# A short-convolution stage in which high and low inputs are one 512-column product per weight tile

## The reference

```python
def short_conv_mixer(h, w_in, conv_w, w_out):
    b_gate, c_gate, u = jnp.split(h @ w_in, 3, axis=-1)
    v = c_gate * u
    y = sum(conv_w[k] * causal_shift(v, CONV_WIDTH - 1 - k) for k in range(CONV_WIDTH))
    return (b_gate * y) @ w_out

def gated_post_add(x, y, g_post, gate, weight):
    return x + weight * gate[:, None, :] * rms_norm(y, g_post)
```

## Time and profile before

| | us |
|---|---|
| runs | 2331.2, 2337.23, 2337.64 |
| median | 2337.23 |
| the profiled execution | 2332.65 |
| its span in the profile | 2330.9 |
| TensorE busy | 2247.9 (96% of the span) |
| VectorE busy | 1524.1 (65%) |
| ScalarE busy | 974.8 (42%) |
| edited stage, first product to last | about 253.6 to 346 |
| mean granted clock of TensorE | 0.976 |

### The profile page before, as it was taken

How to read it: one execution, slowest core, us unless ns; L and a number is a source line. 1 busy time by engine, 2 the same in 40 slices (tenths; PEclk the granted TensorE clock), 3 DMA queues, 4 the chain that set the end, 5 groups by cost and what they waited for, 6 DMA issues and landing times.

```text
span 2330.9 us, 42281 instructions
## 1 busy us (share of the span) xinstructions
PE 2247.9 (96%) x18080; PEld 2211.7 (95%) x18080; DVE 1524.1 (65%) x1704; ACT 974.8 (42%) x957; POOL 145.4 (6%) x269
## 2 busy tenths in 40 slices
PE   6999999999999998799999999999999999999998
PEld 5999999999999998599999999999999999999997
DVE  6876568877457864768867444758985445666554
ACT  3433444434333343543444444334444444334442
POOL 0110001110001100011100000001100000000000
PEclk8999999999789997999999999999999999999999
DMA  9997457995469942049974544548984544444552
GB/s 329 347 340 244 140 184 273 332 326 174 131 212 335 332 139 91 1 164 341 329 244 162 167 137 167 173 160 290 367 293 154 185 140 163 163 157 164 185 181 72
DMA packets 264592, 494.67 MB, mean 212 GB/s; under 512 B 17041, under 2 KB 146449, under 8 KB 264209
## 3 DMA queue, kind: packets, MB, share of 16 engines
q1 hardware_dynamic: 229760, 366.47, 46.7%
q0 software_dynamic: 34704, 126.37, 14.6%
HBM read 491.73 MB, written 1.05 MB: 211 GB/s over the span
## 4 chain that ended last, share of the span: by engine, by line
PE 92%; DVE 3%; ACT 3%; DMA 1%; issue 1%; SPq 0%; DVEq 0%; ACTq 0%
PE PA L469 15%; PE PA L470 15%; PE PA L471 15%; PE PY L469 7%; PE PY L471 7%; PE PY L470 7%; PE PB L469 5%; PE PB L470 5%; PE PB L471 5%; PE PA L519 2%; PE PB L512 2%; DVE wlo L1257 1%; ACT scr L1141 1%; DVE rstd L1299 1%; PE PY L778 1%; DMA mix<-adat 1%
## 5 line engine op out<-in xcount | busy, mean ns | idle before, releaser
L1257 DVE TENSOR_TENSOR wlo<-raw,whi 128x2048 fp32r<-128x2048 f32 x335 | 764.7, 2286 | 449.6 <-ACT whi L936 342.8
L469 PE MATMUL PA<-opA_hi,whi 128*128 128x256 f32 x2528 | 718.0, 284 | 1.8 <-DVE opA_lo L1310 1.8
L470 PE MATMUL PA<-opA_lo,whi 128*128 128x256 f32 x2528 | 716.8, 284 | 0.0
L471 PE MATMUL PA<-opA_hi,wlo 128*128 128x256 f32 x2528 | 716.7, 284 | 0.0
L936 ACT ACTIVATE whi<-raw 128x2048 fp32r<-128x2048 f32 x203 | 384.9, 1901 | 280.3 <-PE PA L471 139.1
L469 PEld LDWEIGHTS PA<-opA_hi,whi 128*128 128x128 f32 x2528 | 486.7, 193 | 2.5 <-issue 2.5
L470 PEld LDWEIGHTS PA<-opA_lo,whi 128*128 128x128 f32 x2528 | 486.8, 193 | 0.1
L471 PEld LDWEIGHTS PA<-opA_hi,wlo 128*128 128x128 f32 x2528 | 486.8, 193 | 0.0
L469 PE MATMUL PY<-opB_hi,whi 128*128 128x256 f32 x1344 | 381.1, 284 | 9.8 <-DVE opB_lo L1368 6.0
L470 PE MATMUL PY<-opB_lo,whi 128*128 128x256 f32 x1344 | 380.3, 283 | 0.0
L471 PE MATMUL PY<-opB_hi,wlo 128*128 128x256 f32 x1344 | 380.3, 283 | 0.0
(11 more groups left out here) (241 smaller groups left out, 2766.4 us busy)
## 6 DMA issues: line engine op xcount, KB each, us to landing
raw<-ffn_w_in SPq DMA_DIRECT2D x176, 512.0 KB, 5.3
mix<-adat POOLq DMA_DIRECT2D x144, 512.0 KB, 6.5
raw<-w_in SPq DMA_DIRECT2D x144, 512.0 KB, 4.7
raw<-w_ff SPq DMA_DIRECT2D x128, 512.0 KB, 4.6
adaw<-adat POOLq DMA_DIRECT2D x96, 512.0 KB, 6.7
raw<-ffn_w_out SPq DMA_DIRECT2D x88, 512.0 KB, 4.6
raw<-w_branch SPq DMA_DIRECT2D x48, 512.0 KB, 4.5
raw<-a_w_in SPq DMA_DIRECT2D x24, 512.0 KB, 4.5
```

What stands on the lines that cost most here:

```text
L469: nc.tensor.matmul(o_, w1, rhs(xh), start=start, stop=False, skip_group_check=True)
L470: nc.tensor.matmul(o_, w1, rhs(xl), start=False, stop=False, skip_group_check=True)
L471: return nc.tensor.matmul(o_, w2_, rhs(xh), start=False, stop=stop, skip_group_check=True)
L1257: TT(wlo[slot][:, 0:w], raw[slot][:, 0:w], whi[slot][:, 0:w].bitcast(F32), ALU.subtract).then_inc(lo_ready, 1)
```

## The change

- The high and low inputs lie in one tensor `op2` [128, 2, 8, 256]; `oph` and `opl` are views of it.
- In the mixer alone, `pair2` takes the place of `mm3`: whi x [in_hi | in_lo] is one product of 512 columns into one bank. wlo x in_hi, 256 columns, is added to the bank's second half. The first half of a bank then holds the main sum, the second the cross sum, so an output tile takes a whole bank instead of half of one.
- A group of 4 output tiles takes four banks: PA and PB for groups 0, 2, 4 and PY for groups 1, 3, 5. `conv_out` takes all eight and waits for all three buffers.
- Every group is evacuated by ScalarE (the cross half, `conv.c0` to `conv.c5`) and then VectorE (adds the main half, `whole`). The loop on ScalarE goes over all six groups. Groups 3 and 5 land in `tmp8`, and the product with c reads that.
- At the boundary behind it ScalarE copies the cross halves into `cb_` (`conv.yc0` to `yc3`), VectorE adds the main halves (`conv.ys0` to `ys3`), and the squares and the update read `cb_`.

```diff
@@ -143,8 +143,9 @@
         x = sb("x", [P, KT, T])
-        oph = {"A": sb("opA_hi", [P, KT, T], F32R), "B": sb("opB_hi", [P, KT, T], F32R)}
-        opl = {"A": sb("opA_lo", [P, KT, T], F32R), "B": sb("opB_lo", [P, KT, T], F32R)}
+        op2 = {"A": sb("opA", [P, 2, KT, T], F32R), "B": sb("opB", [P, 2, KT, T], F32R)}
+        oph = {n: t_[:, 0] for n, t_ in op2.items()}
+        opl = {n: t_[:, 1] for n, t_ in op2.items()}
         tmp8 = sb("tmp8", [P, KT, T])
@@ -167,6 +168,13 @@
         flat = {k: v[:].rearrange("p a b -> p (a b)") for k, v in PS.items()}
+
+        def bank(i):
+            n, j = ("A", i) if i < 2 else ("B", i - 2) if i < 4 else ("Y", i - 4)
+            return flat[n][:, 512 * j:512 * j + 512]
+
+        def halves(n, half):
+            return PS[n][:].rearrange("p (m h) t -> p m h t", h=2)[:, :, half, :]
 
@@ -626,13 +634,40 @@
 
+            def pair2(c, tile, kts, banks, op, before=None, tag=None):
+                pe.wait_ge(lo_ready, c + 1)
+                slot = c % RING
+                for kk, k in enumerate(kts):
+                    if before:
+                        before(k)
+                    for m, b_ in enumerate(banks):
+                        w_ = slice(tile(kk, m), tile(kk, m) + P)
+                        nc.tensor.matmul(bank(b_), whi[slot][:, w_], op2[op][:, :, k, :], start=k == 0, stop=False,
+                                         skip_group_check=True)
+                        last = nc.tensor.matmul(bank(b_)[:, T:2 * T], wlo[slot][:, w_], op2[op][:, 0, k, :], start=False,
+                                                stop=k == KT - 1, skip_group_check=True)
+                        if tag and k == KT - 1 and m in (1, 3, 5):
+                            S(last, f"{tag}.bank{m // 2}")
+                last.then_inc(multiplied, 1)
+
             for g in range(6):
-                buf = "AB"[g % 2]
-                take(buf)
-                group512(CH["conv_in"] + 2 * g, buf, "A", lo_of("01") if g == 0 else None)
-                by(buf, *(("V", f"conv{g}") if g in (3, 5) else ("S", f"conv{g}")))
-            out1024(CH["conv_out"], "B", "01", lambda k: need(pe, "V", f"conv.lo{k // 4}"))
-            by("Y", "V", "01.u7")
+                if g % 2 == 0:
+                    take("A")
+                    take("B")
+                else:
+                    take("Y")
+                for h in range(2):
+                    pair2(CH["conv_in"] + 2 * g + h, tile_in512, range(4 * h, 4 * h + 4),
+                          range(4) if g % 2 == 0 else range(4, 8), "A", lo_of("01") if g == 0 else None)
+                for n_ in ("AB" if g % 2 == 0 else "Y"):
+                    by(n_, "V", f"conv{g}")
+            for n_ in "ABY":
+                take(n_)
+            for q in range(4):
+                pair2(CH["conv_out"] + q, tile_out, (2 * q, 2 * q + 1), range(8), "B",
+                      lambda k: need(pe, "V", f"conv.lo{k // 4}"), tag="01" if q == 3 else None)
+            for n_ in "ABY":
+                by(n_, "V", "01.ysum")
             boundary("01", "02")
@@ -988,7 +1023,15 @@
 
-                if not sub.startswith("b"):
+                if sub == "01":
+                    for q in range(4):
+                        y_there(q)
+                        n_ = "ABYY"[q]
+                        S(AC(cb_[:, 2 * q:2 * q + 2, :], halves(n_, 1)[:, 2 * (q == 3):2 * (q == 3) + 2, :], ACT.Copy), f"conv.yc{q}")
+                    squares(f"{sub}.y", cb_, lambda q: need(act, "V", f"conv.ys{q}"))
+                    root(f"{sub}.y")
+                    prep_to(c_next + 3)
+                elif not sub.startswith("b"):
                     squares(f"{sub}.y", PY, y_there)
@@ -1081,13 +1124,18 @@
             boundary("00", "01", CH["conv_in"], CH["conv_in"])
-            for g in (0, 1, 2, 4):
+            for g in range(6):
                 c = CH["conv_in"] + 2 * g
...
                 act.wait_ge(multiplied, c + 2)
-                dst = cb_ if g < 2 else cc_
                 half_ = g if g < 2 else (g - 2) // 2
-                S(AC(dst[:, 4 * half_:4 * half_ + 4, :], PS["AB"[g % 2]][:], ACT.Copy), f"conv{g}")
+                dst = cb_[:, 4 * half_:4 * half_ + 4] if g < 2 else cc_[:, 4 * half_:4 * half_ + 4] if g in (2, 4) else \
+                    tmp8[:, 4 * half_:4 * half_ + 4]
+                if g % 2 == 0:
+                    S(AC(dst[:, 0:2, :], halves("A", 1), ACT.Copy))
+                    S(AC(dst[:, 2:4, :], halves("B", 1), ACT.Copy), f"conv.c{g}")
+                else:
+                    S(AC(dst, halves("Y", 1), ACT.Copy), f"conv.c{g}")
             prep_to(CH["conv_out"] + 1)
@@ -1320,6 +1368,13 @@
                 prep_to(c_next + 2)
+                ysrc = cb_ if sub == "01" else PY
+                if sub == "01":
+                    for q in range(4):
+                        need(dve, "S", f"conv.yc{q}")
+                        S(TT(cb_[:, 2 * q:2 * q + 2, :], cb_[:, 2 * q:2 * q + 2, :],
+                             halves("ABYY"[q], 0)[:, 2 * (q == 3):2 * (q == 3) + 2, :], ALU.add), f"conv.ys{q}")
+                    seen["V", "01.ysum"] = S.n
                 if not sub.startswith("b"):
@@ -1331,7 +1386,7 @@
                     for k in range(KT):
-                        S(STT(tmp8[:, k, :], PY[:, k, :], G_(sub)[:, k:k + 1], rstd[:], ALU.mult, ALU.mult), f"{sub}.u{k}")
+                        S(STT(tmp8[:, k, :], ysrc[:, k, :], G_(sub)[:, k:k + 1], rstd[:], ALU.mult, ALU.mult), f"{sub}.u{k}")
                         if k > 0:
@@ -1454,14 +1509,27 @@
             need(dve, "G", "cpad")
+            def whole(pos):
+                c = CH["conv_in"] + 2 * pos
+                prep_to(c + 4)
+                need(dve, "S", f"conv.c{pos}")
+                half_ = pos if pos < 2 else (pos - 2) // 2
+                dst = cb_[:, 4 * half_:4 * half_ + 4] if pos < 2 else cc_[:, 4 * half_:4 * half_ + 4] if pos in (2, 4) else \
+                    tmp8[:, 4 * half_:4 * half_ + 4]
+                if pos % 2 == 0:
+                    S(TT(dst[:, 0:2, :], dst[:, 0:2, :], halves("A", 0), ALU.add))
+                    own(S(TT(dst[:, 2:4, :], dst[:, 2:4, :], halves("B", 0), ALU.add), f"conv{pos}"))
+                else:
+                    own(S(TT(dst, dst, halves("Y", 0), ALU.add), f"conv{pos}"))
+
+            whole(0)
+            whole(1)
             for g in range(2):
                 pos = 3 + 2 * g
-                c = CH["conv_in"] + 2 * pos
-                prep_to(c + 4)
-                dve.wait_ge(multiplied, c + 2)
-                need(dve, "S", f"conv{pos - 1}")
+                whole(pos - 1)
+                whole(pos)
                 ts = range(4 * g, 4 * g + 4)
-                own(S(TT(cv_[:, 4 * g:4 * g + 4, 2:258], PB[:], cc_[:, 4 * g:4 * g + 4, :], ALU.mult), f"conv{pos}"))
+                own(S(TT(cv_[:, 4 * g:4 * g + 4, 2:258], tmp8[:, 4 * g:4 * g + 4], cc_[:, 4 * g:4 * g + 4, :], ALU.mult)))
                 for t in ts:
...
```

More of the change, by code:

```diff
@@ L668, in _ @@
             take("A")
-            bh, bl = (oph["B"][:].rearrange("p a b -> p (a b)"), opl["B"][:].rearrange("p a b -> p (a b)"))
+            bh, bl = (oph["B"].rearrange("p a b -> p (a b)"), opl["B"].rearrange("p a b -> p (a b)"))
             for kv in range(2):
@@ L1111, in _ @@
                 S(AC(vtok[br], t3(flat["Y"][:, n_ * 512:n_ * 512 + 512], 2), ACT.Copy), "vtok")
-            bh = oph["B"][:].rearrange("p a b -> p (a b)")
+            bh = oph["B"].rearrange("p a b -> p (a b)")
             tf = tmp8[:].rearrange("p a b -> p (a b)")
@@ L1203, in _ @@
                 need(act, "V", q_ + "rety2")
-                S(AC(oph["B"][:], tmp8[:], ACT.Copy), q_ + "rhi")
+                S(AC(oph["B"], tmp8[:], ACT.Copy), q_ + "rhi")
                 group("p0", 10, "B", half(1, 0), ACT.Copy)
@@ L1220, in _ @@
                 act.wait_ge(multiplied, c + 32)
-                S(AC(oph["B"][:], tmp8[:], ACT.Copy), q_ + "shi")
+                S(AC(oph["B"], tmp8[:], ACT.Copy), q_ + "shi")
                 group("h11", 17, "B", half(0, 1), ACT.Sigmoid, ("V", q_ + "m0.1"))
@@ L1226, in _ @@
                 act.wait_ge(multiplied, c + 40)
-                S(AC(oph["B"][:], tmp8[:], ACT.Copy), q_ + "phi")
+                S(AC(oph["B"], tmp8[:], ACT.Copy), q_ + "phi")
                 group("h21", 21, "B", half(0, 1), ACT.Sigmoid, ("V", q_ + "m1.1"))
@@ L1486, in _ @@
             tf = tmp8[:].rearrange("p a b -> p (a b)")
-            bh, bl = (z["B"][:].rearrange("p a b -> p (a b)") for z in (oph, opl))
+            bh, bl = (z["B"].rearrange("p a b -> p (a b)") for z in (oph, opl))
             dve.wait_ge(cmp_in, 64)
@@ L1650, in _ @@
                 need(dve, "S", q_ + "rhi")
-                S(TT(opl["B"][:], tmp8[:], oph["B"][:].bitcast(F32), ALU.subtract), q_ + "rlo")
+                S(TT(opl["B"], tmp8[:], oph["B"].bitcast(F32), ALU.subtract), q_ + "rlo")
                 prep_to(c + 25)
@@ L1687, in _ @@
                 need(dve, "S", q_ + "shi")
```

(4 more changed lines are left out.)

## The result

The changed kernel takes 2349.97 us in the median (2341.4 to 2352.62, 7 runs) against 2334.83 of the kernel before in the same runs (2328.85 to 2337.64): a ratio of 1.0062, 95% interval 1.0042 to 1.0081, so 14.5 us slower (10 to 19). The forecast was slower by 8.8 us, 2343.7 with a range of 2337 to 2352. Sign and range held; some 60% of the size was named. The changed kernel once more (e5_after_again) has 2347.0 us against 2333.02: 1.0054 (1.0034 to 1.0073).

The account below looks back on a forecast made before the run. TensorE, never stopping in the edited stage, was taken as the bound. Costs of 13.8 us less gains of 5.0 us gave net +8.8 us, so 2343.7 us, with a range of 2337 to 2352.

Parts of the forecast that it names:

- Step 4: Ahead of conv_out: TensorE stops for VectorE's add of group 5, queued behind a late conv.hi0; +8.35 us.
- Step 1: Mixer tiles: one 512-column product replaces two of 256; a tile takes 0.3375 us, a gain of 22.5 ns.
- Step 5: After the stop ahead of conv_out: TensorE's clock falls and some 5.2 us run at half speed; +2.6 us.
- Step 7: Boundary behind conv_out: ScalarE copies four cross halves first and all four squares come after; +2.45 us.
- Steps 2 and 3: Groups 0 to 3: evacuation hidden, 2.9 us gained. Group 4: copy and add delay chunk 10, +0.4 us.
- Step 6: Group 5 and conv_out's products: 32 and 64 cheaper tiles, nothing else ending later; 2.2 us gained.
- The second of cover at chunk 17: Chunk 17's split would end at T5+31.2, TensorE at T5+32.6; without that cover at most 0.6 us on the path.
- no gain in width: Rival: the wide product costs 0.240 us, so only costs remain, +13.8 us, 2348.7 us; chance 0.19.
- Cheapest pair: Rival: a tile takes 0.325 to 0.330 us, both weight loads hidden; +6.0 us, 2340.9 us; chance 0.17.
- free width: Rival: the wide product costs a weight load, 0.120 us, a tile 0.240 us; -13.1 us, 2321.8 us; chance 0.04.
- the stop was made as read: Rival denied this: TensorE waits only for group 5's copy and add, 2.5 us; +0.3 us, 2335.2; chance 0.05.

Follow-up runs that it names:

- e1_hi0_early: The changed kernel with ScalarE writing conv.hi0 right behind the copy of group 4, not of group 5; ratio 1.0018 to the kernel before, stop 2.53 us.
- e9_late_hi0: The kernel before, with ScalarE made to wait for the end of group 5 ahead of conv.hi0; stop 2.50 us, stage 112.31 us.
- after: The profiled execution of the changed kernel, nothing else edited; 2352.62 us.
- e7_double_wide: The changed kernel with the second product of a tile also 512 columns wide; a tile takes 0.453 us, the profiled execution 2371.86 us.
- e6_front_wide: The wide product in groups 0 to 2 alone, the rest as in the kernel before; 2333.71 us, ratio 1.0002, stage 106.61 us.
- e2_no_pool_adds: The changed kernel with POOL's three adds to x at the boundary behind the mixer made by VectorE; one profiled execution, 2339.91 us.
- e8_interleave: e1_hi0_early with ScalarE's copies and squares at the boundary interleaved, two squares behind the last copy; one profiled execution, 2347.74 us.

## Why the prediction was right, and where it was not

- **Step 4, the stop.** Right in mechanism, order and size: 8.29 us against 8.35, ended by the add that was named. e1_hi0_early and e9_late_hi0 show that it has two causes that only together make it long: without the late `conv.hi0` 2.5 us are left, and with it alone it is 2.5 us as well.
- **Step 1, the price of the wide product.** The mis-sized term. The step took the 0.2175 us of a float32 record with 256 columns as that of one product with 512; measured are 0.230 or 0.2367, and a tile of 0.3467 or 0.3533, not 0.3375; the 0.3533 of 96 of the 256 tiles in after, and of 160 in e5_after_again, lies outside the 0.330 to 0.350 of the forecast. The gain is 13.3 or 6.7 ns a tile and not 22.5. The measured price also lies over both figures that the prediction quotes for this product, 216 and 131 ns. float32r pays 13.3 ns a product whatever its width (e7_double_wide), the float32 record 4. The stage's own spacing of 0.120 us for 256 columns had this number in it: 0.1067 for the columns and 0.0133 over. A row of the same kind of operand, split into a part for columns and a fixed part, was the nearer one. With 13.3 ns the sum would have been 13.8 - 3.0 = +10.8, close to the 11.6 measured, but in part by luck: the clock of step 5 cost 1.0 less than forecast and the boundary of step 7 1.5 more.
- **Steps 2 and 3.** Evacuation through both engines is hidden in groups 0 to 3, as said: TensorE has no stop there; e6_front_wide shows it for groups 0 to 2 without the rest. Chunk 10's wait cost +0.30 (forecast +0.4); TensorE idled for 0.56 us and not for 1, since its dearer tiles brought it there later.
- **Step 5, the clock.** Fell in the stop and came back, but sooner: low from 326.0 to 332.8, of which 3.4 us are busy, a cost of 1.6 us against 2.6. In e5_after_again it was low from 323.4, and 4.5 us of that busy. The restarts of the earlier trace rows were the upper end. One of its falls was misread: a mean clock of 0.81 between two levels of 1.0 and 0.5 puts it at 35.6 and not 35.8, so 2.2 us into the idle stretch and not 2.4; nothing in the sum hung on it.
- **Step 6.** -0.13, and -0.4 for the 64 tiles of conv_out, against -2.2: the same error as step 1.
- **Step 7, the boundary.** +3.96 against +2.45. To the reciprocal it was +2.7, of which the detour that was argued is 2.1 and the clock, counted at nothing, 0.7: TensorE's idle stretch there was 1.84 us and the clock fell after it (0.66 in 356 to 361), though I took 2.4 us as the shortest. In e2_no_pool_adds, with the same lines up to there and the clock up, it takes 4.62 us from the end of conv_out to the reciprocal, in after 5.29, before 2.56. The detour was 2.1 and not 2.45 partly because the four squares behind the last copy took 2.18 us and not 2.40. The other +1.2 was missed outright: `ysrc` moves the scalings' input from PSUM to SBUF, where they meet POOL's adds. The step only asked how long the operations are, not what runs beside them. The second of cover at chunk 17 held: its split ended at T5+31.4, 1.2 us ahead of the end of conv_out.
- **Rivals.** Of the forecast gain a tile, 60% was there in tiles of 0.3467 us and 30% in those of 0.3533. In the time of the whole execution no gain in width (2348.7) came nearest to the 2349.97, but that is luck: the boundary and the attention stage brought it there. Cheapest pair and free width are out; the stop was made as read.
- **What the prediction lacked:** the attention stage's clock. Executions of one kernel differ by 6 to 7 us between its two levels. The two pairs of times of the kernel before were its mark, and I took their middle for granted in the kernel after. It and the terms above brought the median 6 us over the forecast, near the upper end of the range.

## What to carry to other kernels

Before lengthening a loop over evacuations, list what stands behind it on that engine: a copy that waits for the end of a group makes everything behind it wait, here an operand that had been ready 9 us earlier, and with it a whole queue on the next engine. Where a step moves an operand from PSUM to SBUF, ask who else reads SBUF in that stretch. And before trading instructions for width, split the price of one into a part per column and a fixed part from rows of the same operand type: here only 13 ns of 120 could be saved.

## What the hardware showed beyond that

- A tile of one wide and one narrow product costs 0.3467 or 0.3533 us, and changes between the two only where TensorE had stopped: in after 0.3467 until the wait for chunk 10 and 0.3533 after it, in e5_after_again the other way round. All of the difference lies behind the wide product (0.2300 or 0.2367 us to the next start; 0.1167 behind the narrow one in both). Tiles of three 256-column products gave 0.360 at full clock in every run that has them. What sets it wasn't found.
- Whether a short stop lets the clock fall isn't settled by its length: 2.53 us ahead of conv_out left it up in e1_hi0_early and let it fall in e8_interleave, 1.83 us at the boundary left it up in e2_no_pool_adds and let it fall in e1_hi0_early.
- The attention stage runs at 1.2 GHz for 27 to 61 us, in executions of kernels whose lines there are the same, and is some 0.3 us longer for each us of it.
